# Inverse rms of two norms made once per token on 88 partitions, in a one-core encoder step

## The reference, cut to what matters

```
x += 0.5 * SwiGLU(RMSNorm(x))          # FFN1, hidden width 2816
h  = RMSNorm(x);  x += mixer(h)        # gated convolution beside a 4-head mLSTM, one output projection
x += 0.5 * SwiGLU(RMSNorm(x))          # FFN2
y  = RMSNorm(x)
RMSNorm(x) = x * rsqrt(mean(x*x over the 1024 features) + 1e-6) * gain
```

## Time and profile before

| | us |
|---|---|
| median of 3 runs | 2047.66 |
| lowest, highest | 2047.12, 2047.93 |
| the profiled execution's own time | 2047.06 |
| its span | 2044.9 |
| TensorE busy in it | 2002.8 |
| VectorE busy | 910.1 |
| ScalarE busy | 504.0 |
| GpSimd busy | 90.5 |

### The profile page before, as it was taken

The page is one execution under the profiler, slowest core; times in us unless marked ns, Lnnn a source line. Parts: engine busy times, 40 slices in busy tenths (PEclk is TensorE's granted clock), DMA queues, the critical chain, the costliest instruction groups (busy, mean ns, idle before and its releaser), DMA issues.

```text
span 2044.9 us, 31002 instructions
## 1 busy us (share of the span) xinstructions
PE 2002.8 (98%) x12520; PEld 1984.6 (97%) x12520; DVE 910.1 (45%) x1559; ACT 504.0 (25%) x896; POOL 90.5 (4%) x145
## 2 busy tenths in 40 slices
PE   7999999999999998999999999999999999999998
PEld 6999999999999998999999999999999999999998
DVE  5533333333333238612677758534333432343344
ACT  5211111121112124333444524211211110121122
POOL 1000000000000013200000012000000000000001
PEclk9999999999999999999999999999999999999999
DMA  6011101110111011211111332011101101110102
GB/s 209 21 42 62 62 21 41 62 62 21 41 62 55 7 50 68 65 52 32 33 41 31 106 99 62 20 43 62 47 15 61 62 26 35 62 62 21 51 1 85
DMA packets 144177, 105.09 MB, mean 51 GB/s; under 512 B 6376, under 2 KB 136248, under 8 KB 144120
## 3 DMA queue, kind: packets, MB, share of 16 engines
q1 hardware_dynamic: 143992, 104.26, 16.5%
q10 hardware_dynamic: 128, 0.03, 0.0%
HBM read 95.36 MB, written 8.92 MB: 51 GB/s over the span
## 4 chain that ended last, share of the span: by engine, by line
PE 93%; DVE 5%; ACT 1%; issue 1%; DMA 0%; ACTq 0%; DVEq 0%; POOL 0%
PE bank L204 30%; PE bank L210 29%; PE bank L209 29%; PE bank L208 1%; PE bank L206 1%; DVE ffn_normed L171 1%; DVE in_lo L163 1%; PE bank L643 0%; PE bank L2011 0%; DVE ffn_root_work L143 0%; PE bank L2025 0%; PE bank L2024 0%; PE bank L867 0%; PE bank L2027 0%; DMA vector_rows<-in_cache_conv 0%
## 5 line engine op out<-in xcount | busy, mean ns | idle before, releaser
L204 PE MATMUL bank<-in_hi,w_hi 128*128 128x352 f32 x2256 | 738.3, 327 | 8.5 <-DVE in_lo L717 3.4
L210 PE MATMUL bank<-in_hi,w_lo 128*128 128x352 f32 x2256 | 730.6, 324 | 0.0
L209 PE MATMUL bank<-in_lo,w_hi 128*128 128x352 f32 x2256 | 727.6, 323 | 0.0
L204 PEld LDWEIGHTS bank<-in_hi,w_hi 128*128 128x128 f32 x2256 | 425.6, 189 | 13.1 <-issue 5.4
L209 PEld LDWEIGHTS bank<-in_lo,w_hi 128*128 128x128 f32 x2256 | 427.6, 190 | 1.2
L210 PEld LDWEIGHTS bank<-in_hi,w_lo 128*128 128x128 f32 x2256 | 427.7, 190 | 0.0
L400 DVE TENSOR_TENSOR ffn_hidden<-ffn_silu,bank 128x352 f32<-128x352 f32 x132 | 68.8, 521 | 671.2 <-PE bank L210 581.0
L204 PE MATMUL bank<-ffn_hidden_hi,ffn_w_hi_more 128*128 128x352 f32 x1056 | 342.1, 324 | 2.5 <-ACT ffn_hidden_hi L347 2.1
L411 DVE SCALAR_TENSOR_TENSOR x<-bank,x 128x352 f32<-128x352 f32 x528 | 267.7, 524 | 161.7 <-PE bank L210 112.1
L210 PE MATMUL bank<-ffn_hidden_hi,ffn_w_lo_more 128*128 128x352 f32 x924 | 297.7, 322 | 0.0
L209 PE MATMUL bank<-ffn_hidden_lo,ffn_w_hi_more 128*128 128x352 f32 x924 | 297.2, 322 | 0.0
(11 more groups left out here) (227 smaller groups left out, 1496.8 us busy)
## 6 DMA issues: line engine op xcount, KB each, us to landing
raw<-in_ffn_w_gate SPq DMA_DIRECT2D x44, 512.0 KB, 3.9
ffn_raw_more<-in_ffn_w_down SPq DMA_DIRECT2D x44, 512.0 KB, 5.5
raw<-in_w_in SPq DMA_DIRECT2D x24, 512.0 KB, 3.8
raw<-in_ffn_w_up SPq DMA_DIRECT2D x22, 512.0 KB, 4.9
ffn_raw_more<-in_ffn_w_up SPq DMA_DIRECT2D x22, 512.0 KB, 5.4
x_parked<-x SPq DMA_DIRECT2D x3, 1408.0 KB, 5.6
x<-x_parked SPq DMA_DIRECT2D x3, 1408.0 KB, 9.9
raw<-in_w_out SPq DMA_DIRECT2D x8, 512.0 KB, 4.2
```

The costliest lines, as they stand in the source:

```text
L204: pe.matmul(out, w_hi, in_hi, start=first, stop=False)
L209: pe.matmul(out, w_hi, in_lo, start=False, stop=False)
L210: return pe.matmul(out, w_lo, in_hi, start=False, stop=last)
```

## The change

The mean square of a token is made once, not on 128 partitions. With PIECES = 4 and PIECE = 88, four matmuls give the 352 means as an 88x4 array. VectorE adds epsilon there (88x4), GpSimd raises it to the power -0.5 (88x4), and four matmuls by an identity of 88 spread the result over 128 partitions and 352 tokens; VectorE copies that bank to `inv_rms` (128x352). The reciprocal, the square root and the Newton step are gone.

```
+PIECES = 4
+PIECE = BLK // PIECES
 def norm_add(pool, sh, n):
 ...
+    pool.wait_ge(sh.root_step, 2 * n + 1)
+    if n:
+        pool.wait_ge(sh.roots_spread, n)
+    pool.tensor_tensor(sh.norm.roots, sh.norm.means, sh.minus_half[0:PIECE, :].to_broadcast([PIECE, PIECES]), ALU.pow
+                       ).then_inc(sh.root_ready, 1)
 def norm_stats(pe, sh, n, bank):
     pe.wait_ge(sh.square_added, (n + 1) * KT)
     if n:
-        pe.wait_ge(sh.root_step, 4 * (n - 1) + 1)
-    pe.matmul(bank[:, 0:BLK], sh.mean_all[:, :], sh.norm.square_sum[:, :],
-              start=True, stop=True).then_inc(sh.stats_done, 1)
+        pe.wait_ge(sh.root_step, 2 * n)
+    for i in range(PIECES):
+        last = pe.matmul(bank[0:PIECE, i:i + 1], sh.norm.square_sum[:, i * PIECE:(i + 1) * PIECE],
+                         sh.mean_all[:, 0:1], start=True, stop=True)
+    last.then_inc(sh.stats_done, 1)
+def norm_spread(pe, sh, n, bank):
+    pe.wait_ge(sh.root_ready, n + 1)
+    for i in range(PIECES):
+        last = pe.matmul(bank[:, i * PIECE:(i + 1) * PIECE], sh.norm.roots[:, i:i + 1].to_broadcast([PIECE, P]),
+                         sh.ident[0:PIECE, 0:PIECE], start=True, stop=True)
+    last.then_inc(sh.roots_spread, 1)
+def norm_means_dve(dve, sh, n, bank):
+    dve.wait_ge(sh.stats_done, n + 1)
+    if n:
+        dve.wait_ge(sh.root_ready, n)
+    dve.tensor_scalar(sh.norm.means, bank[0:PIECE, 0:PIECES], EPS, None, ALU.add).then_inc(sh.root_step, 1)
+def norm_roots_dve(dve, sh, n, bank):
+    dve.wait_ge(sh.roots_spread, n + 1)
+    if n:
+        dve.wait_ge(sh.scaled, KT * n)
+    dve.tensor_copy(sh.norm.inv_rms[:, :], bank[:, 0:BLK]).then_inc(sh.root_step, 1)
+    dve.wait_ge(sh.root_step, 2 * n + 2)
```

Norms 0 and 1 move into the rounds of blocks 1 and 2 themselves. On VectorE (`last` is the last pair):

```
+                    if last and b:
+                        norm_means_dve(dve, sh, out_norm + b - 1, gate_bank[0])
+                    if first and b == 0 and own_norm is not None:
+                        norm_means_dve(dve, sh, own_norm, down_bank[0])
                     hidden_of(r, 1)
+                    if first and b == 0 and own_norm is not None:
+                        norm_roots_dve(dve, sh, own_norm, down_bank[0])
+                    if last and b:
+                        add_down(r, b, range(4))
+                        norm_roots_dve(dve, sh, out_norm + b - 1, gate_bank[0])
+                        def add_between(k):
+                            if k in (2, 4, 6, 7):
+                                add_down(r, b, ({2: 4, 4: 5, 6: 6, 7: 7}[k],))
+                        norm_split_dve(dve, sh, out_norm + b - 1, out_gain, add_between)
+                        continue
```

ScalarE's part of the split follows `hidden_act(r, 1)` in the same rounds, with the squares of the round's own block in between; on TensorE the means come after `gate_up` and the spread between d = 3 and d = 4 of `down`:

```
+                if last and b and not tail:
+                    norm_spread(pe, sh, out_norm + b - 1, gate_bank[0])
                 for d in range(4, KT):
```

Norm 2's mean moves one tile earlier in the mixer, its spread is where the mean was. The mixer's wait for all of `x_added` stays. In the output projection the means of norms 3 and 4 come after (block 1, d = 3) and (block 2, d = 1), their spreads one tile later, and VectorE's splits hold adds in between: the last three of block 1 in norm 3's split, the fourth and fifth of block 2 in norm 4's:

```
+        for d in range(4):
             o.add(dve, 1, d)
+        norm_means_dve(dve, sh, NORM_FFN2, sh.bank[3])
+        o.add(dve, 1, 4)
+        norm_roots_dve(dve, sh, NORM_FFN2, sh.bank[3])
+        norm_split_dve(dve, sh, NORM_FFN2, V_FFN2, second_adds)       # adds 5, 6, 7 before k = 5, 6, 7
         dve.wait_ge(o.x_in[2], 16)
+        o.add(dve, 2, 0)
+        o.add(dve, 2, 1)
+        norm_means_dve(dve, sh, NORM_FFN2 + 1, sh.bank[3])
+        o.add(dve, 2, 2)
+        norm_roots_dve(dve, sh, NORM_FFN2 + 1, sh.bank[3])
+        norm_split_dve(dve, sh, NORM_FFN2 + 1, V_FFN2, third_adds)    # adds 3, 4 before k = 3, 7
```

Norm 5's mean is made after the first gate and up tiles of FFN2's first round, into down_bank[0], its spread before the second up tile, and TensorE's first `down` matmul waits for VectorE's copy:

```
+                    if first and own_norm is not None and (b, j, w) == (0, 1, "up"):
+                        pe.wait_ge(sh.root_step, 2 * own_norm)
+                        norm_spread(pe, sh, own_norm, down_bank[0])
...
+                        if first and own_norm is not None and (b, j, d) == (0, 0, 0):
+                            pe.wait_ge(sh.root_step, 2 * own_norm + 2)
```

More of the change, by code:

```diff
@@ L75, in norm_buffers @@
     norm.root_work = sb("root_work", [P, BLK], FP32)
+    norm.means, norm.roots = norm.mean_square[0:PIECE, 0:PIECES], norm.root_work[0:PIECE, 0:PIECES]
     norm.inv_rms = sb("inv_rms", [P, BLK], FP32)
@@ L168, in norm_split_dve @@
         i = n * KT + k
+        if also is not None:
+            also(k)
         if i >= 3:
@@ L364, in body @@
                         norm_squares(act, sh, out_norm, s.x_added, (r - 1) * 8)
-                    if last and b == 2:
-                        norm_act_squaring(act, sh, out_norm, s.x_added, (r - 1) * 8)
                     if first and b == 1 and own_norm is not None:
-                        norm_act(act, sh, own_norm)
+                        norm_split_act(act, sh, own_norm)
                     if first and b < 2 and head:
@@ L380, in body, with square @@
                     hidden_act(r, 1)
+                    if last and b == 2 and following:
+                        act.wait_ge(s.up_done, ROUNDS * 2)
+                        following.late_high(act)
+                    if last and b:
+                        def square(k):
+                            act.wait_ge(s.x_added, r * 8 + k + 1)
+                            norm_square(act, sh, out_norm + b, k)
+                        norm_split_act(act, sh, out_norm + b - 1, square)
             loop(act, body)
[L383 to L385 removed]
             if tail:
                 tail.act_end(act)
[L388 to L390 removed]
         @block.vector
@@ L426, in body @@
                         continue
-                    if last and b == 2:
-                        norm_dve(dve, sh, out_norm, gate_bank[0], out_gain)
                     if first and b == 1 and own_norm is not None:
-                        norm_dve(dve, sh, own_norm, gate_bank[1], gain)
+                        norm_split_dve(dve, sh, own_norm, gain)
                     if first and b < 2 and head:
@@ L457, in gate_up @@
                         pe.wait_ge(read, step - 1)
[L458 to L462, removed]
+                    if first and own_norm is not None and (b, j, w) == (0, 1, "up"):
+                        pe.wait_ge(sh.root_step, 2 * own_norm)
+                        norm_spread(pe, sh, own_norm, down_bank[0])
                     if last and b == 2 and j == 0 and w == "gate" and not tail:
-                        pe.wait_ge(sh.root_step, out_norm * 4 + 1)
+                        pe.wait_ge(sh.root_step, 2 * out_norm + 2)
                     if b == 0:
@@ L479, in gate_up @@
                     done.then_inc(s.gate_done if w == "gate" else s.up_done, 1)
+                    if first and own_norm is not None and (b, j, w) == (0, 0, "up"):
+                        norm_stats(pe, sh, own_norm, down_bank[0])
                     if last and b and tail:
@@ L521, in body @@
                     gate_up(pair, r, b, 1, first, last)
-                    if first and b == 0 and own_norm is not None:
-                        pe.wait_ge(sh.root_step, (own_norm - 1) * 4 + 1)
                     if last and b and not tail:
@@ L623, in _ @@
             pool.wait_ge(mean_ready, t + 1)
-            pool.tensor_tensor(root, mean, minus_half[part, :], ALU.pow).then_inc(root_ready, 1)
+            pool.tensor_tensor(root, mean, sh.minus_half[part, :], ALU.pow).then_inc(root_ready, 1)
         pool.wait_ge(const, n)
@@ L2184, in _ @@
                     o.finish_mixer(pe, d // 7)
-                if d == 3 and b:
+                if (b, d) in ((1, 3), (2, 1)):
                     norm_stats(pe, sh, NORM_FFN2 + b - 1, sh.bank[3])
+                if (b, d) in ((1, 4), (2, 2)):
+                    norm_spread(pe, sh, NORM_FFN2 + b - 1, sh.bank[3])
 def encoder_kernel(nc, args, outs):
```

79 lines of the change are left out of this document (30 added, 49 removed).

## The result

| | before | after |
|---|---|---|
| time, median | 2047.12 us (2045.98 to 2047.93, 5 runs) | 2034.58 us (2034.37 to 2035.07, 5 runs) |
| ratio | | 0.994, 95% interval 0.993 to 0.9951 |
| profiled execution, its span | 2047.06, 2044.9 us | 2035.07, 2033.3 us |

The change made the kernel 12.5 us faster, where 2048.5 (2043.5 to 2052.9) was forecast. First, what the forecast was about, in TensorE's timeline of the kernel after (start, length, instruction, idle time before it and its releaser). L132 are the means, L142 the spread, L201 a product. All of it starts 5.9 us earlier than in the earlier trace rows, which is already the first sign that something else has happened.

The account below looks back on a forecast made before the run. TensorE was taken as the bound, busy 2002.8 of 2044.9 us. A gain of 0.5 up to the mixer's block 1 and a loss of 1.3 by FFN2 gave +0.8 us: 2047.9, as median 2048.5, range 2043.5 to 2052.9.

Parts of the forecast that it names:

- TensorE's own work: Mean 0.7 and spread 1.0 us per norm where the mean took 0.59: 1.1 us more per norm on the path.
- VectorE and GpSimd: Per norm, a copy of 0.525 us and an 88x4 addition of 0.17 on VectorE, a power of 0.6 on GpSimd.
- its cover: 24 matmuls (3.83 us) between mean and spread, said to cover even a power of 2.3 us plus addition and handovers.
- End of FFN1: Gaps there go, a wait of some 8 us for adds takes their place, mixer starts at 805.4 (802.5 to 806.6).
- The gaps: TensorE's waits of 1.14, 2.72 and 1.87 us around norms 0 and 1 at the end of FFN1, forecast to go.
- The clock behind the long wait: One fall of TensorE's clock after the mixer's 8 us wait, costing 1.0 to 2.1 us, taken as 1.6.
- rival A: Slower, by clock falls after the mixer's and FFN2's new waits: 2052.9 us; sign, mixer's block 0 over 15 us; chance 0.17.
- FFN2: First `down` waits 2.6 us for VectorE's copy of norm 5's roots; loss up to there 1.3 us (0.3 to 2.3).
- The norm stretch as a whole: From norm 0's mean to FFN2's round of block 1, all six norms: a loss of 0.8 us.
- the fall that went: The old second clock fall, after norm 1's 2.04 us gap at the mixer's start, which cost 1.6 us after 819.08.
- Sum: -0.5 + 1.3 = +0.8 us on the profiled 2047.06, so 2047.9; 2048.5 as median, no change that can be told.
- B: Faster, as VectorE reaches the last add early: 2042.2 us; sign, mixer start below 802.5; chance 0.14.

Follow-up runs that it names:

- e2: Kernel after with minus_half and gate_bias as two columns of one tensor, so later tiles lie where they lay before: 2046.48 us, ratio 1.0003.
- e7: Kernel after with VectorE's copy of the roots ahead of hidden tile j = 1 in each FFN's first rounds: 2030.93 us, ratio to before 0.9926.
- e8: Kernel after with the mixer's wait in two parts, norm 2's small matmuls two tiles later, and a last low half made earlier: 2026.33 us, ratio 0.9905.
- e1: Kernel before with one unused tile that puts later buffers 32 bytes higher, nothing of the change: 2033.82 us, ratio 0.9943.
- e10: Kernel before with a stream of product triples at various start offsets put behind its end, other engines idle: 247 us more in one execution.
- e13: Kernel before with streams at its end, all starts 0 modulo 64, odd triples, small matmuls or waits between: 158.8 to 161.1 ns a matmul, one execution.
- e5: Kernel before with unused tiles so that only the hidden tiles of both FFNs start at a multiple of 64 bytes: 2042.47 us, ratio 0.9981.
- e6: Kernel before with unused tiles so that only the extra weight tiles of both FFNs start at a multiple of 64 bytes: 2044.94 us, ratio 0.9996.
- e11: Kernel before with unused tiles so that extra weight and hidden tiles of both FFNs start at a multiple of 64 bytes: 2036.64 us, ratio 0.9953.
- e12: Kernel before with two unused tiles, one ahead of `x`, so that all tiles the FFN's products read start at 32 modulo 64: 2035.12 us, ratio 0.9944.

## Why the prediction was wrong

Point by point:

- **TensorE's own work.** Right: the records of mean and spread span 0.71 and 1.02 us, forecast 0.7 and 1.0. Measured as the forecast measured the old mean, to one step of 0.16 before the second product behind it (those start at 758.11 and 762.83), they cost the path 0.66 and 0.90. By the Trainium skill, "TensorE: Matmul & The Clock Gate", section LDWEIGHTS, the estimate was 0.59 and 0.85; the trace lies 0.07 and 0.05 above it.
- **VectorE and GpSimd.** The copy took 0.52 and split operations beside GpSimd's additions 1.24 to 1.26, as forecast; the power took 1.03 us and not 0.6, within its cover.
- **End of FFN1.** Right up to the mixer's start. In times from norm 0's mean, TensorE was to reach the mixer's wait at 34.1 and leave it at 42.2; it did at 34.0 (791.25) and 41.9 (799.22), a wait of 7.97 against 8.1. The gaps went, and the one before block 1 too.
- **The clock behind the long wait.** Too small. The forecast had one fall of 1.6 us; 0.54 over 7 us is 3.2, and the mixer's block 0 took 15.9 us from its start (before: 14.35), so the sign that rival A named, over 15 us, came. Block 1 started 57.9 us after norm 0's mean (before: 55.9; forecast with its fall: 57.0). The size is not fixed: behind the same wait of 8.0 us the clock was 0.54, 0.70 and 0.77 over 7 us in after, e2 and e7.
- **FFN2.** The wait was 2.29 us, forecast 2.6. The clock behind it fell to 0.74, which rival A had and the forecast had not: the 48 matmuls took 9.3 us, against 7.6 in e7. By a rule of the Trainium skill, "TensorE: Matmul & The Clock Gate", section "The HAM clock gate", the lower level is the default that activity lifts. The long wait agrees with it. The short one had a fall in the kernel after and none in e8, so no run here shows from which wait on it comes.
- **The norm stretch as a whole.** +0.9 us in the trace of after, forecast +0.8, but that is luck: each of the two falls cost some 1.6 us more than the forecast had, and the mixer from block 1 to norm 3's mean took 391.8 us where it had taken 395.2. Of these 3.4 us the forecast had 1.6 (the fall that went); most of the rest is a higher clock over 920 to 970 us, 0.97 against 0.93. At the old placement, in e2's trace, the stretch took 1291.96 - 762.2 = 529.8 us, +3.4. (e1, with the old norms at the new placement, took 524.5, so after lost 2.7 against it.) These are single executions (before's 526.3 was 526.0 in e10 and in e13, which have its instructions), and e2's is the slowest of its ten; over all its runs the ratio is 1.0003, with an interval of -1.4 to +2.5 us.
- **Sum.** This failed. It added up changes at the norms and let every other matmul stand at its old pace ("-0.5 + 1.3 = +0.8 us on the profiled execution's 2047.06"), and no rival moved any of them either. The missing term is the 32 bytes by which one moved tile of one column shifts the FFNs' tiles: -12.4 us in e1 (0.5 to 0.7% of 12,500 matmuls of 160 ns). The diff showed the line; I read it as a constant with no cost.
- **Rivals.** B had the direction, faster, but not by this cause: its sign, a mixer start below 802.5 (39.3 us after norm 0's mean), did not come (41.9).

What is shown: the placement causes the gain (e1, e2), all of it needs both groups of tiles (e5, e6, e11), likeness and not the multiple of 64 is what counts (e12), no other engine is needed for it (e10), and the pace is carried (e10, e13, and the rounds of the kernel before, whose like tiles ran at 160.0 and at 161.1). What stays open: why FFN loops with like tiles stayed at 158.9 and never at 161.1 in after, e1, e11 and e12, though waits and small matmuls stand ahead of them, and what part of the chip holds the state. e12 is the only kernel whose product tiles are all alike at a start other than 0.

## What to carry to other kernels

When a diff adds, drops or resizes an on-chip tile, write down which later tiles move and by how much, and in a kernel that TensorE bounds put a term of some 0.5% in either direction into the range for it (here it was 0.6%). Before believing an A/B difference of that size, run the old kernel with an unused tile that reproduces the new addresses; here it returned the whole of a gain that would have been credited to the norms. And a forecast new wait is a place to edit: moving two things past the waits that this change made was worth another 10 to 11 us.

## What the runs showed of the hardware

- Matmuls of 128x128 by 128x352 back to back took 158.9, 160.0, 161.1 or 162.2 ns with the clock at 1.00 and every other engine idle. At one set of addresses three of these occurred (158.9, 160.0, 161.1), each held from the second dozen matmuls to the end of the stream.
- Tiles that start alike modulo 64 bytes, at 0 or at 32, gave 1260 matmuls in 200 us in every such kernel; unlike ones 1248 to 1254.
- A float32 power of 88x4 on GpSimd took 1.03 us, of 128x1 0.57.
- A wait of 2.29 us at the same place was followed by a clock of 0.74 over 5 us in one kernel and 1.00 in another. One of 8.0 us was followed by 0.54, 0.70 and 0.77 over 7 us in three.
